# Hybrid mixer and expert kernel: half-feature projection chunks, grouped narrow columns, unnormed tokens transposed, GLA exponents after the last maxima

## What is computed

```python
# first block
c_act = silu(c)
sh1, sc1, ... = split(c_act @ ada_w + ada_b)             # modulation
h = rmsnorm(x, norm1_g) * (1.0 + sc1) + sh1
proj = h @ w_in                                           # gdn_qkv, gdn_z, gdn_b, gdn_a, ssd_z, ssd_xbc, ssd_dt
xbc = silu(causal_dwconv(ssd_xbc, ssd_conv_w) + ssd_conv_b)
dt = softplus(ssd_dt + ssd_dt_bias); beta = sigmoid(gdn_b)
g = -exp(gdn_a_log) * softplus(gdn_a + gdn_dt_bias)
x = x + g1 * mixer(...);  x = x + g2 * moe_ffn(...)       # 32 experts, 4 of them for a token
x = rmsnorm(x, final_g)
# second block
u = rms_norm(x, g_mix);  z = u @ w_in_2
y_a = nsa_attention(z ...); y_b = gla_attention(z ...)    # softmax branches; decayed linear attention
log_a = log_sigmoid(a_low @ w_a2 + b_a) / 16;  b = cumsum(log_a)   # exponents of GLA
x = x + mixed @ w_out;  x = x + hier_moe(rms_norm(x, g_ffn))       # 32 experts, 2 of them for a token
return rms_norm(x, g_final)
```

## Time and profile before

| | us |
|---|---|
| median of 3 runs | 2130.63 |
| lowest, highest | 2130.08, 2131.89 |
| the profiled execution's own time | 2130.74 |
| its span in the profile | 2129.0 |

### The profile page before, as it was taken

How to read it: one execution, slowest core, us unless ns; L and a number is a source line. 1 busy time by engine, 2 the same in 40 slices (tenths; PEclk the granted TensorE clock), 3 DMA queues, 4 the chain that set the end, 5 groups by cost and what they waited for, 6 DMA issues and landing times. The chain is left out here.

```text
span 2129.0 us, 24746 instructions
## 1 busy us (share of the span) xinstructions
PE 1953.1 (92%) x10258; PEld 917.4 (43%) x10258; DVE 501.1 (24%) x1041; ACT 322.6 (15%) x576; POOL 82.1 (4%) x184
## 2 busy tenths in 40 slices
PE   6989999989999999999999999899899878778786
PEld 4677665643333333333333333345454422223232
DVE  2255544432122112221211211322342200000000
ACT  2134421210000000000000000213341100000001
POOL 2011031000000000000000000100020000000000
PEclk9999999999999999999999999999999899999999
DMA  9332167589999999999999999935254799999996
GB/s 338 121 129 80 49 243 260 225 341 427 428 428 428 428 428 428 428 428 428 428 428 428 428 428 428 362 119 171 62 202 172 286 428 428 428 428 428 428 428 274
DMA packets 98567, 707.15 MB, mean 332 GB/s; under 512 B 12315, under 2 KB 17933, under 8 KB 61517
## 3 DMA queue, kind: packets, MB, share of 16 engines
q1 hardware_dynamic: 98508, 706.36, 80.9%
HBM read 705.29 MB, written 1.05 MB: 332 GB/s over the span
## 5 line engine op out<-in xcount | busy, mean ns | idle before, releaser
L1707 PE MATMUL ps<-ring,arena 128*64 128x512 f32 x1536 | 337.5, 593 | 11.8 <-DMA ring<-in_moe_w_gu 11.8
L2932 PE MATMUL ps<-ring,arena 128*32 128x512 f32 x768 | 173.7, 616 | 42.5 <-DMA ring<-in_w_up 23.5
L1707 PEld LDWEIGHTS ps<-ring,arena 128*64 128x64 f32 x1536 | 109.8, 137 | 234.0 <-issue 206.5
L1734 PE MATMUL ps<-ring,arena 128*64 128x512 f32 x768 | 168.9, 592 | 0.0
L2155 PE MATMUL ps<-ring 128*128 128x512 f32 (+1 forms) x320 | 139.5, 586 | 0.7 <-ACT ring L2543 0.6
L1758 ACT ACTIVATE arena<-arena 128x512 f32<-128x512 f32 x32 | 20.1, 629 | 760.0 <-DVE arena L1789 760.0
L2932 PEld LDWEIGHTS ps<-ring,arena 128*32 128x32 f32 x768 | 52.6, 113 | 162.7 <-issue 160.4
L1707 PE MATMUL ps<-arena 128*64 128x512 f32 x512 | 113.5, 593 | 4.5 <-DMA arena<-in_moe_w_gu 4.5
L1079 PEld LDWEIGHTS ps<-arena 128*128 128x128 f32 x832 | 101.1, 200 | 35.3 <-issue 32.7
L1079 PE MATMUL ps<-arena 128*128 128x128 f32 x832 | 109.1, 289 | 2.3 <-DVE arena L1071 1.3
L1734 PEld LDWEIGHTS ps<-ring,arena 128*64 128x64 f32 x768 | 54.9, 137 | 109.9 <-issue 100.2
(11 more groups left out here) (601 smaller groups left out, 1989.0 us busy)
## 6 DMA issues: line engine op xcount, KB each, us to landing
ring<-in_moe_w_gu SPq DMA_DIRECT2D x96, 2048.0 KB, 28.4
ring<-in_moe_w_down SPq DMA_DIRECT2D x48, 2048.0 KB, 31.3
arena<-in_moe_w_gu SPq DMA_DIRECT2D x32, 2048.0 KB, 28.4
ring<-in_w_up SPq DMA_DIRECT2D x24, 2048.0 KB, 19.8
ring<-in_w_gate SPq DMA_DIRECT2D x24, 2048.0 KB, 26.9
ring<-in_w_down SPq DMA_DIRECT2D x24, 2048.0 KB, 27.0
ring<-in_w_in SPq DMA_DIRECT2D x22, 2048.0 KB, 8.2
arena<-in_moe_w_down SPq DMA_DIRECT2D x16, 2048.0 KB, 33.6
```

Source lines behind the costliest of these rows:

```text
L1707: last = M.matmul(ps[halves[j], 4 + which, :], xgT[buf][:, k, CAP * ee:CAP * ee + CAP], w[:, k2, at:at + 512], start=False, stop=(k == KD ...
L1734: last = M.matmul(ps[halves[j], 6, :], yT[:, k % KH, halves[k // KH]], w[:, k % KH, 512 * j:512 * j + 512], start=False, stop=(k == 2 * KH ...
L2932: last = M.matmul(ps[quads[e], 4 + which, :], xgT[:, k, quads[e]], w[e][:, k, :], start=(k == 0), stop=(k == KD - 1))
```

## The change

First stage. The ring order becomes `ada` 0, `ada` 1, xBC 0, xBC 1, `ada` 2, `ada` 3, xBC 2. Units 0 to 7 are split: a first half over k = 0 to 3, then, later, a second half over k = 4 to 7. Two units share a bank (u and u + 4 in banks 2, 3, 0, 1), so units 4 to 7 start without the start flag and their second halves wait for the convolution of u - 4. ACT copies transposed features 4 to 7 out of PSUM unmodulated (`s_xh`), and DVE modulates them in SBUF. The modulation sums of chunk 2 stand between the first halves of units 6 and 7, those of chunk 3 after them. The narrow columns are computed ahead of the gate units, with the 32 columns as the weights and 256 tokens streaming, in four column groups (eight matmuls); ACT copies the four partial sums (`narrow_parts`), and after the first two gate units PE adds and transposes them with `pick` (two matmuls). ACT's sigmoid, exp and ln stand between gate unit 13 and 14.

Second mixer. POOL multiplies `mg` by `fg` during the first expert stage. DVE writes PSUM times that product to `un`, unnormed, and PE transposes it; the reciprocal root comes in later, as the per-token `scale` of ACT's `take_unit`. The squares, the `fg` products and the residual's scaling go behind the transposes; units use banks 4, 5, 0, 1, 2, 3. In step 7 DVE does the maxima first and the GLA exponents after them.

```diff
-    for i, j in enumerate((0, 2, 1, 3)):
-        ra.add(cols(ada_w, 512 * j), (KD, 512), (s_ada, i + 1), i)
-    for j in range(3):
...
+    add_early(0)
+    add_early(1)
+    add_xbc(0)
+    add_xbc(1)
+    add_early(2)
+    add_early(3)
+    add_xbc(2)
...
+    def unit_bank(u):
+
+        if u < 8:
+            return ps[:, (2, 3, 0, 1)[u % 4], T * P * (u // 4):T * P * (u // 4) + T * P]
+        return ps[:, (6, 7, 4, 5)[u - 8], 0:T * P]
...
+            def half_unit(u, w, half):
+                for k in range(4 * half, 4 * half + 4):
+                    if u == 0:
+                        pe.wait_ge(s_hk, k + 1)
+                    last = M.matmul(unit_bank(u), w[:, k, (u % 4) * P:(u % 4 + 1) * P], hT[:, k, :], start=(k == 0 and not 4 <= u < 8),
+                                    stop=(k == KD - 1), skip_group_check=True)
+                if half:
+                    last.then_inc(s_unit, 1)
...
+            modulation_sums(pe, cond, 5)
+            spread(1)
+            w = [ra.take(pe), None]
+            pe.wait_ge(s_xh, 2)
+            for u in range(8):
+                if u == 2:
+                    pe.wait_ge(s_hk, 4)
+                if u == 4:
+                    pe.wait_ge(s_rows, 48)
...
+                    w[1] = ra.take(pe)
+                half_unit(u, w[u // 4], 0)
+                if u == 6:
+                    modulation_sums(pe, cond, 4)
+            spread(2)
+            modulation_sums(pe, cond, 5)
+            spread(3)
+            for u in range(8):
+                if u >= 4:
+                    pe.wait_ge(s_conv, u - 3)
+                half_unit(u, w[u // 4], 1)
+            pe.wait_ge(s_cw, 3)
+            w = ra.take(pe)
+            for u in range(8, 12):
+                half_unit(u, w, 0)
+                half_unit(u, w, 1)
+            pe.wait_ge(s_small, 16 * 7)
+            pe.wait_ge(s_conv, 7)
+            for r in range(2):
+                for g in range(4):
+                    last = M.matmul(ps[32 * g:32 * g + 32, 0, 0:T * P], wsm[:, 4 * r + g, :], hT[:, 4 * r + g, :],
+                                    start=(r == 0), stop=(r == 1))
+            last.then_inc(s_nr, 1)
...
+                if n == 0:
+                    pe.wait_ge(s_conv, 8)
+                    pe.wait_ge(s_const, 2)
+                    pe.wait_ge(s_npt, 1)
+                    for t in range(T):
+                        last = M.matmul(ps[:, 1, NE * t:NE * t + NE], narrow_parts[:, t * P:(t + 1) * P], pick[:, 0:NE])
+                    last.then_inc(s_nr, 1)
...
+                pool.wait_ge(s_p8, 32)
+                G.tensor_tensor(mg, fg, mg, ALU.mult).then_inc(s_fmg, 1)
...
-                A.activation(z[:, t, 512 * j:512 * j + n], ps[:, bank, 0:n], ACT.Copy).then_inc(s_zt2, 1)
+                A.activation(z[:, t, 512 * j:512 * j + n], ps[:, bank, 0:n], ACT.Copy, scale=ssx[:, 2 + t:3 + t]).then_inc(s_zt2, 1)
...
+            A.activation(squares[:, 1, :], banks(2, 2, D), ACT.Square, accum_out=ssx[:, 1:2]).then_inc(s_fs, 1)
             act.wait_ge(s_pT, 1)
             A.activation(posT, ps[:, 7, 0:36], ACT.Copy).then_inc(s_pTt, 1)
             act.wait_ge(s_uT, 1)
...
+            act.wait_ge(s_un, 1)
+            A.activation(squares[:, 0, :], banks(0, 2, D), ACT.Square, accum_out=ssx[:, 0:1]).then_inc(s_fs, 1)
             act.wait_ge(s_uT, 2)
...
+            dve.wait_ge(s_fmg, 1)
+            V.tensor_tensor(un[:, 0, :], banks(0, 2, D), mg, ALU.mult).then_inc(s_un, 1)
+            dve.wait_ge(s_fs, 1)
+            V.tensor_tensor(un[:, 1, :], banks(2, 2, D), mg, ALU.mult).then_inc(s_un, 1)
```

161 lines of the change are left out of this document (76 added, 85 removed).

## The result

| | median, us | runs, us | profiled run, us | its span | granted clock |
|---|---|---|---|---|---|
| before | 2130.49 | 2130.08 to 2131.89 | 2130.74 | 2129.0 | 0.971 |
| changed | 2103.47 | 2100.95 to 2108.45 | 2103.48 | 2101.8 | 0.981 |

The ratio is 0.9882 (95% interval 0.9857 to 0.9906): 25 us, 20 to 30 by the interval. The forecast was 2108, from 2104 to 2116. The two profiled runs differ by 27.2 us of span; the sum had 23.1. The rest of this document is about the four us between, and about 3.4 us that are hidden in them with the other sign.

A forecast was written before the change was run, and what follows sets the result against it. The prediction took the expert stages as bound by DMA weight streams and the mixers by PE. Its parts, 0 - 6.8 - 2.8 - 7.5 - 6.0 = -23.1 us, gave 2107.6 from 2130.74, taken as 2108, range 2104 to 2116.

The forecast's parts named there:

- the sum: Whole kernel: the gains of all four parts with their clock terms, 0 - 6.8 - 2.8 - 7.5 - 6.0 = -23.1 us.
- Part 2: First stage, narrow columns ahead of the gates: -6.8 us, and -2.8 us of clock in the next block's first unit.
- part 3: Start of the second mixer, tokens transposed unnormed: -7.5 us with the clock, -5.2 without.
- part 4: Attention step 7, maxima ahead of the exponents: -6.0 us, -4.5 without the clock.
- the rival with a chance of 0.25: Clock falls despite short waits in two or three places: 6.6 us back, 2114.3, or 2111 to 2114 in part; chance 0.25.
- No part failed to be handed on: Rival: something with its own time takes up one of the three gains, 5 to 7 us: 2113 to 2117; chance 0.13.
- neither stream absorbed anything: Rival: expert weights already DMA-bound before each stage, so an earlier start gives nothing: 2126 to 2131; chance 0.04.
- second pass: Rival: over 32 tokens at one expert, second expert stage run again, about 438 us more, near 2546; chance 0.01.
- Part 1: First stage, half-feature units: nothing, within 1.5 us either way; the stretch 50.5 us against 50.6.
- The row for a kept clock: Ground for full clock after short waits: PE waited 1.11 us at 393.81 with the clock at 1.00 throughout.
- Both expert stages as long as before: Sign: both expert stages keep their length, each only shifted, 9 to 10 us the first, 23 the second.
- the rival that had this case with a chance of 0.04: Rival "more than I count": under 2104, from waits that shrink behind the three places; chance 0.04.

The follow-up runs named there:

- The kernel with fillers in the first stage only: The changed kernel plus four matmuls whose result nobody reads, in PE's four waits of the first stage; 2102.66 us, ratio 0.9881 to the kernel before.

## Why the prediction was right, and where not

**Part 2, 3 and 4: mechanism and size as forecast.** Behind gates the block end costs 0.95 us (forecast 0.94), the narrow matmuls 1.07 + 0.53 (0.96 + 0.46), and nothing of the DVE and ACT chain shows. The 1.07 for four column groups of 256 columns is nearer to the 0.96 worked out from L275 than to 1.45; it is 3.2 times less than a plain unit's 3.45. The Trainium skill (TensorE: Matmul & The Clock Gate, Part 3) reports a factor of 2.38 for three column tiles, from which the 1.45 came; the measurement decides against carrying that factor over to four groups. The chain of part 3 was forecast by adding rows of other places, and gave 6.66 us for 6.5; that of part 4 gave 4.41 for 4.5. A take with a scale by token lasts 0.69 us instead of 0.60, and PE waits for none. By the Trainium skill (ScalarE: Activation LUTs, What ACT_TABLE_LOAD costs), with some 93 ns for a pointer operand, the trace agrees, at 90 ns. The clock stayed up in all three (2.64, 0.92, 1.40 us for 2.8, 1.0, 1.5), so the rival with a chance of 0.25 didn't come in these places. No part failed to be handed on, neither stream absorbed anything, and there was no second pass.

**Part 1: the step that failed.** The prediction put 50.5 us for the stretch, with waits of 1.0 and 0.9 for DVE's first features and of 0.73 for ACT's copy. The stretch takes 50.98 at full clock, 0.5 more, half of it from the waits (1.20, 0.97 and 0.72); the weights arrived, and DVE's lag was not felt. The term that was missing is the clock: the prediction asked after every one of its other short waits whether the clock stays, and didn't ask it here, where the work around the wait is thin (spreads of one column, 1.05 us, between waits of 0.72 and 1.20 us). It cost 3.1 us, and the stretch came out 3.6 above its sum, outside the stated 1.5. The row for a kept clock, the wait of 1.11 us ahead of 393.81, came true for part 2 and 3 and was no proof for part 1, as the table of spells shows.

**The 8 us that weren't forecast.** "Both expert stages as long as before" was right for the streams (391.5 and 391.6 us) and wrong for the ends. What this 8 us is made of, the runs tell apart only in part.

The 1.57 us up to the block behind the GDN units look like a gain of part 2: from the next block's first unit to there all nine profiles with the narrow columns ahead of the gates have 143.06 us, the four without have 147.27, 147.23, 144.54 and 144.53. But 1.48 us of the two shorter ones are the slow first unit (5.17 for 3.69), and what is left is 143.06 again. The two longer ones lose 2.64 on the first unit and 1.57 more at one place, behind a wait of 2.44 us that all thirteen have; timelines of PE, the kernel before and then the one with the maxima alone:

```profile
174.90 2.08 PE L588 MATMUL ps<-arena 128*128 128x512 f32 x2 [2.44 <-ACT arena L703]
```

```profile
175.09 1.13 PE L588 MATMUL ps<-arena 128*128 128x512 f32 x2 [2.44 <-ACT arena L703]
```

In the first the granted clock is 0.50 from about 174.5 to 178, in the second it stays at 1.00. So this piece is a spell as well, which part 2's nine profiles didn't draw and two of the other four did.

The others, too, are spells that come or not in the same code, but for the 0.39 us of the first expert stage, which nothing explains. In the GLA part PE's timelines read, before and changed:

```profile
1576.72 5.40 PE L2374 MATMUL ps<-ring,arena 128*128 128x512 f32 x8
```

```profile
1554.25 3.70 PE L2433 MATMUL ps<-ring,arena 128*128 128x512 f32 x8
```

The kernel with fillers in the first stage only, which has the changed kernel's code from there on, has it at 5.40 again; its stretch from the first mixer's out projection to the first expert matmul takes 53.03 us and its second stage 463.06, as in the profile of before (53.04 and 462.80), where the changed kernel has 51.68 and 459.62. And the kernel before ran from 2120.6 to 2132.8 us in later runs. So of the 27.2 us between the two profiles, 22.5 less 3.4 are terms of the sum, 7.6 are spells that the two profiled runs happened to draw or not, and 0.4 stay unexplained. The medians' 25 us, with an interval of 20 to 30, can't tell how much of this is lasting. That the total came so near to its forecast is in part luck: a loss and a gain that nobody forecast stand against each other. And the result under 2104 is not the rival that had this case with a chance of 0.04, since what was won beyond the sum are spells and not waits. What decides whether a spell comes wasn't settled: why the same code behind the same wait, a few microseconds earlier or later, has it or has it not stays open.

## What to carry to other kernels

Where a change replaces one long wait by several short ones, sum the work at full clock and then put a spell of half clock for each short wait into the range (here 1.4 to 1.7 us each), above all where the work around it is thin, or a matmul without a reader into the wait (it helped in the first stage and in the second mixer, little or nothing elsewhere). Solid work on both sides made a spell rarer here, not impossible: a wait of 2.44 us between projection units drew one in 2 of 13 profiles. A stage that is bound by its stream hides such spells except at its first and last piece, so a profile's gain in it is to be checked against the stream's own length before it is credited to the edit. And a term is best costed from a row of the same shape: all terms that had one came within 0.3 us.

## What the runs showed of the hardware

The clock fell at waits of 0.97 to 1.2 us where the work ahead was thin, and the clock that was missing came in steps: 0, 1.71 or 3.4 us in the first stage of thirteen profiles, nothing between. The same code with the same waits drew one spell or two, and the same wait of 2.44 us between solid units drew one in two profiles and none in eleven. Matmuls whose result is never read kept the clock at 1.00 through the first stage in three kernels, and cost nothing there, being shorter than the wait (0.23 us left of 1.20). Around the rank sums of the second mixer they did so in three kernels (5.12 us of missing clock in the changed kernel, 0 with them), around those of the first mixer in none (3.41, 1.71 and 3.41 us). In the second expert stage 391.5 us passed between the first and the last awaited arrival in all five kernels looked at, whatever PE did between. Sixteen 128x128 transposes ran at full clock, in 2.29 us, behind a wait of 1.06 us; with the clock at 0.50 the same sixteen took 3.67.
